# Feed-forward stages whose first chunk multiplies unnormalised x: a two-block transformer kernel

## What is computed

```python
def rmsnorm(x, g):
    x32 = x.astype(jnp.float32)
    y = x32 * lax.rsqrt(jnp.mean(x32 * x32, axis=-1, keepdims=True) + RMS_EPS)
    return y.astype(x.dtype) * g

def modulate(z, g, shift, scale):
    return rmsnorm(z, g) * (1.0 + scale) + shift

def swiglu(h, wi, wo):
    a, u = jnp.split(h @ wi, 2, axis=-1)
    return (jax.nn.silu(a) * u) @ wo

x = x + 0.5 * m[2] * swiglu(modulate(x, norm_g[l, 0], m[0], m[1]), ffn1_wi[l], ffn1_wo[l])
```

## Time and profile before

| what | value |
|---|---|
| median of 3 runs | 3235.24 us (3233.91 to 3236.90) |
| profiled execution | 3234.64 us |
| its span in the trace | 3232.1 us |
| PE busy | 3152.3 us, 98% of the span |
| DVE busy | 1860.3 us, 58% |
| ACT busy | 1026.0 us, 32% |
| share of PE in the chain that ended last | 89% |

### The profile page before, as it was taken

The page is one execution under the profiler, slowest core; times in us unless marked ns, Lnnn a source line. Parts: engine busy times, 40 slices in busy tenths (PEclk is TensorE's granted clock), DMA queues, the critical chain, the costliest instruction groups (busy, mean ns, idle before and its releaser), DMA issues.

```text
span 3232.1 us, 37291 instructions
## 1 busy us (share of the span) xinstructions
PE 3152.3 (98%) x15190; PEld 2528.8 (78%) x15190; DVE 1860.3 (58%) x2673; ACT 1026.0 (32%) x1480; POOL 10.2 (0%) x23
## 2 busy tenths in 40 slices
PE   8999999998899999999999999999999998899998
PEld 7888888776678888788877888788887764578887
DVE  7876555645555554666646554566665655554444
ACT  4212222345442222322234222332224344332222
POOL 0000000000000000000000000000000000000000
PEclk9999999999999999999999999999999999899999
DMA  6433432210034433255522443235551210123331
GB/s 229 140 118 124 149 125 85 66 44 11 1 124 152 154 124 117 85 207 190 197 92 79 169 144 131 79 118 206 190 178 62 76 55 1 56 91 102 97 98 52
DMA packets 101846, 365.03 MB, mean 113 GB/s; under 512 B 11247, under 2 KB 12543, under 8 KB 101421
## 3 DMA queue, kind: packets, MB, share of 16 engines
q1 hardware_dynamic: 100636, 357.94, 32.4%
q0 software_dynamic: 1040, 4.71, 0.4%
HBM read 360.51 MB, written 2.10 MB: 112 GB/s over the span
## 4 chain that ended last, share of the span: by engine, by line
PE 89%; DVE 6%; ACT 3%; issue 1%; DMA 1%; SPq 0%; POOL 0%; DVEq 0%; ACTq 0%; POOLq 0%
PE ps L192 25%; PE ps L194 25%; PE ps L193 25%; PE ps L196 4%; PE ps L197 2%; DVE SQ L610 1%; PE ps L496 1%; DVE HL L599 1%; DVE WL L184 1%; PE ps L2373 1%; ACT WH L179 1%; PE ps L2606 0%; DVE XT L855 0%; DVE RAW L1317 0%; PE ps L2706 0%
## 5 line engine op out<-in xcount | busy, mean ns | idle before, releaser
L192 PE MATMUL ps<-HH,WH 128*128 128x512 f32 x2464 | 973.8, 395 | 4.2 <-ACT S L769 2.2
L194 PE MATMUL ps<-HH,WL 128*128 128x512 f32 x2464 | 960.9, 390 | 0.0
L193 PE MATMUL ps<-HL,WH 128*128 128x512 f32 x2464 | 960.0, 390 | 0.0
L179 ACT ACTIVATE WH<-RAW 128x1024 fp32r<-128x1024 f32 x456 | 459.1, 1047 | 622.4 <-PE ps L194 366.5
L184 DVE TENSOR_TENSOR WL<-RAW,WH 128x1024 fp32r<-128x1024 f32 x456 | 542.9, 1219 | 92.3 <-ACT WH L179 92.1
L192 PEld LDWEIGHTS ps<-HH,WH 128*128 128x128 f32 x2464 | 462.9, 188 | 116.7 <-issue 9.9
L194 PEld LDWEIGHTS ps<-HH,WL 128*128 128x128 f32 x2464 | 462.7, 188 | 98.7
L193 PEld LDWEIGHTS ps<-HL,WH 128*128 128x128 f32 x2464 | 463.1, 188 | 97.1 <-issue 4.6
L855 DVE SCALAR_TENSOR_TENSOR XT<-ps,DER,XT 128x512 f32<-128x512 f32 x512 | 346.4, 682 | 249.0 <-PE ps L194 234.2
L192 PE MATMUL ps<-GH,WH 128*128 128x512 f32 x1056 | 412.5, 391 | 4.8 <-DVE GL L793 4.8
L194 PE MATMUL ps<-GH,WL 128*128 128x512 f32 x1056 | 411.1, 389 | 0.0
(11 more groups left out here) (356 smaller groups left out, 2467.8 us busy)
## 6 DMA issues: line engine op xcount, KB each, us to landing
RAW<-in_w_modt SPq DMA_DIRECT2D x200, 512.0 KB, 5.0
RAW<-in_ffn_wi SPq DMA_DIRECT2D x176, 512.0 KB, 4.8
RAW<-in_ffn_wo SPq DMA_DIRECT2D x88, 512.0 KB, 4.9
RAW<-in_w_gu SPq DMA_DIRECT2D x88, 512.0 KB, 4.3
RAW<-in_w_in SPq DMA_DIRECT2D x44, 512.0 KB, 3.6
RAW<-in_w_down SPq DMA_DIRECT2D x44, 512.0 KB, 4.2
RAW<-in_w_out SPq DMA_DIRECT2D x16, 512.0 KB, 4.4
STG<-in_w_modt SPq DMA_DIRECT2D x10, 512.0 KB, 12.8
```

The lines of the kernel that those rows point to most:

```text
L179: act.e.activation(u.hi, u.ld.view, ACT.Copy).then_inc(u.hi_done.sem, 1)
L192: pe.e.matmul(out, wh, x[0], start=first, stop=False)
L193: pe.e.matmul(out, wh, x[1], start=False, stop=False)
L194: m = pe.e.matmul(out, wl, x[0], start=False, stop=last)
```

## The change

Before feed-forward stages 2, 3, 5 and 8, chunk 0 no longer waits for the norm. It multiplies x * a (a: the norm's weights times 1 + scale) as soon as each block of x is final, and three things are put right afterwards: the per-token factor R = 1/rms is multiplied on behind PSUM, and the shift b enters as b times the weights, one number for each output feature. All other chunks still use the normalised h.

- `AheadSplit(k)` splits x * a into `UH` (ACT, 128x512) and `UL` (DVE, 128x512). It stands one step behind the addition of block k: in the last `Down` group of stage 2, in `OutMM` of mixers 1 and 7, in `PoolAdd` of mixer 4.
- `Sums` with `full` adds all eight squares on DVE; `Factor` sums over partitions with one float32 product of 128x512 behind block 2 of chunk 0 and runs `Newton` on 128x512. `NormSplit` stands behind it and reads R from SBUF.
- `Up` of chunk 0: DVE multiplies both halves by R, ACT applies SiLU with the bias, DVE adds the other bias and multiplies. Chunk 1 takes the two halves in turns as well.
- `BiasDot`, `BiasSum`, `BiasCopy` make the bias numbers a stage ahead: two more weight loads, eight DVE operations on 128x256, two PE products of one column, an ACT copy.
- `OutMM` uses six banks in place of three, the weights of the following stage are split at d = 5 and 6 in place of both at d = 7.
- In the four stages the condition is spread behind chunks 2 and 3, and the dot products are dealt out from chunk 4 on.
- `RstdSum`, `RstdSpread` and the `Busy` products go at these four places.

```diff
+class AheadSplit(Step):
+    def scalar(self, act):
+        P, k = self.P, self.k
+        act.wait_ge(*self.ready)
+        act.wait_ge(*self.gain)
+        act.e.activation(P.UH[:, k, :], P.XT[:, k, 0:T], ACT.Identity, scale=P.mod_a(self.mi, k)).then_inc(self.hi.sem, 1)
+    def vector(self, dve):
+        P, k = self.P, self.k
+        dve.wait_ge(*self.hi)
+        dve.e.scalar_tensor_tensor(P.UL[:, k, :], P.XT[:, k, 0:T], P.mod_a(self.mi, k), P.UH[:, k, :].bitcast(F32),
+                                   ALU.mult, ALU.subtract).then_inc(self.lo.sem, 1)
+class Factor(Step):
+    def sum(self, pe):
+        P = self.P
+        pe.wait_ge(*self.total)
+        pe.wait_ge(*self.bankfree)
+        pe.e.matmul(P.banks[7], P.ONE, P.SA[:, 0:T], start=True, stop=True).then_inc(self.summed.sem, 1)
+class BiasDot(Step):
+        for k in range(8):
+            w, b = self.view[:, :, k * 128:(k + 1) * 128], P.mod_b(self.mi, k)
+            if k == 0:
+                dve.e.tensor_scalar(P.ACC, w, b, None, ALU.mult).then_inc(self.part[k].sem, 1)
+            else:
+                dve.wait_ge(*self.part[k - 1])
+                dve.e.scalar_tensor_tensor(P.ACC, w, b, P.ACC, ALU.mult, ALU.add).then_inc(self.part[k].sem, 1)
...
 (Up.tensor)
+                    if self.factor and k == 2:
+                        self.factor.sum(pe)
...
 (Up.scalar)
+                if q == 0 and self.factor:
+                    act.wait_ge(*self.scaled[q])
+                    act.wait_ge(*self.biased)
+                    act.e.activation(s, s, ACT.Silu, bias=P.BIAS[:, q:q + 1]).then_inc(self.silu[n].sem, 1)
...
 (Up.vector)
+                if self.factor:
+                    d = F.S[:, 1, :] if q else s
+                    dve.wait_ge(*self.done[q, n])
+                    dve.wait_ge(*self.factor.done)
+                    dve.wait_ge(*self.sfree[n])
+                    dve.e.tensor_tensor(d, out, self.factor.R, ALU.mult).then_inc(self.scaled[q].sem, 1)
+                    if q:
+                        dve.wait_ge(*self.silu[n])
+                        dve.wait_ge(*self.scaled[q])
+                        dve.wait_ge(*self.biased)
+                        dve.e.scalar_tensor_tensor(s, d, P.BIAS[:, q:q + 1], s, ALU.add, ALU.mult).then_inc(self.mul[n].sem, 1)
...
 (OutMM)
-        self.b = d % 3
+        self.b = (0, 1, 2, 4, 5, 6, 4, 5)[d]
...
 (ffn)
+            if ahead:
+                self.downfree = NONE
+                F = Ffn(self, ctx, mi, segs, self.norm_tiles(ctx, False))
+                R = self.sb(ctx, self.name("RB"), [128, T], F32)[:, :]
+                units, self.units = self.units, self.split([wi[1], wi[NF + 1]])
+                F.factor = self.add(Factor(self, R))
+                self.add(NormSplit(self, mi, segs, F.h, after, R=R))
+                self.add(Up(F, 0, units))
...
                     for d in range(8):
                         self.add(DownPart(down, d))
+                        if nxt is not None and last and d:
+                            self.add(AheadSplit(self, nxt, d - 1, down.evac[d - 1, 0][0]))
...
 (out_products)
+        for d in range(8):
+            ahead = self.split([w[d + 1]]) if d < 7 else None
+            if d in (5, 6):
+                later += self.split([following[d - 5]])
+            job(d)[1](units)
+            units = ahead
...
+                if d == 1:
+                    bias["lds"] = self.bias_loads(wi)
+                elif d == 2:
+                    bias["dot"] = self.add(BiasDot(self, nxt, bias["lds"]))
...
 (mixer_pool)
-            self.add(Busy(self, 4))
             last = add(3)
+            self.add(SumsEnd(sums))
+            self.add(AheadSplit(self, mi + 1, 7, last.evac))
```

More of the change, by code:

```diff
@@ L408, in late @@
     def late(self, dve, k):
-        if 1 < k < 7:
+        if 1 < k < (9 if self.full else 7):
             P, w, j = self.P, self.w, k - 1
@@ new lines, with __init__, vector @@
+class BiasDot(Step):
+    def __init__(self, P, mi, lds):
+        self.P, self.mi, self.lds = P, mi, lds
+        self.before, self.shift = P.biased, P.modt[mi, 0]
+        self.part = [P.s["bias_dve"].next() for _ in range(8)]
+        self.summed = P.s["bias_mm"].next()
+        for ld in lds:
+            ld.users = [self.part[7]]
+        at = [ld.slot for ld in lds]
+        lo, step = min(at), abs(at[0] - at[1])
+        self.view = P.RAW[:, lo:lo + step + 1:step, :]
+        self.order = [at.index(lo), 1 - at.index(lo)]
+    def vector(self, dve):
+        P = self.P
+        for ld in self.lds:
+            dve.wait_ge(*ld.landed)
+        dve.wait_ge(*self.before)
+        dve.wait_ge(*self.shift)
+        for k in range(8):
[5 more added lines that the diff above has]
+                dve.e.scalar_tensor_tensor(P.ACC, w, b, P.ACC, ALU.mult, ALU.add).then_inc(self.part[k].sem, 1)
@@ new lines, with __init__, tensor, scalar @@
+class BiasSum(Step):
+    def __init__(self, dot, bank=7):
+        self.dot, self.bank = dot, bank
+    def tensor(self, pe):
+        P, dot = self.dot.P, self.dot
+        pe.wait_ge(*dot.part[7])
+        for i, q in enumerate(dot.order):
+            m = pe.e.matmul(P.banks[self.bank][:, 508 + q:509 + q], P.ACC[:, i, :], P.ONE[:, 0:1], start=True, stop=True,
+                            skip_group_check=True)
+        m.then_inc(dot.summed.sem, 1)
+class BiasCopy(Step):
+    def __init__(self, dot, bank=7):
+        self.dot, self.bank = dot, bank
+        dot.P.biased = self.done = dot.P.s["bias_act"].next()
+    def scalar(self, act):
+        P = self.dot.P
+        act.wait_ge(*self.dot.summed)
+        act.e.activation(P.BIAS, P.banks[self.bank][:, 508:510], ACT.Copy).then_inc(self.done.sem, 1)
@@ L3043, in norm_split, with bias_loads, ffn @@
         return h
-    def ffn(self, mi, segs, wi, wo, after, following, blk=None, rows=(), early=()):
+    def bias_loads(self, w):
+        return [self.add(LoadStep(Load(self, src))).ld for src in (w[0], w[NF])]
+    def ffn(self, mi, segs, wi, wo, after, following, blk=None, rows=(), early=(), ahead=False, nxt=None, dot=None):
         with self.scope() as ctx:
@@ L3182, in add @@
             def add(g):
-                return [self.add(PoolAdd(self, mi, means[g], o, bfree, sums)) for o in range(2)][1]
+                for o in range(2):
+                    k = 2 * g + o
+                    adds[k] = self.add(PoolAdd(self, mi, means[g], o, bfree, sums))
+                    if k:
+                        self.add(AheadSplit(self, mi + 1, k - 1, adds[k - 1].evac))
+                return adds[k]
             prod(0)
```

138 lines of the change are left out of this document (107 added, 31 removed).

## The result

| what | before | after |
|---|---|---|
| median, runs of the same chip | 3235.37 us (3233.91 to 3236.90, 4 runs) | 3252.65 us (3250.44 to 3255.11, 4 runs) |
| profiled execution, its span | 3234.64 us, 3232.1 us | 3255.11 us, 3253.3 us |
| PE, DVE, ACT busy | 3152.3, 1860.3, 1026.0 us | 3140.5, 1914.0, 1047.9 us |

The account below looks back on a forecast made before the run. PE, busy 98% of the span, bounds the kernel. Chunk 2 starts +2.3, bias products +1.9, `OutMM` waits +5.1 and clock +11.8 make +21 on 3234.6: 3255.7, with 0.6 for the median 3256 us; range 3232 to 3272.

Parts of the forecast that it names:

- The start of a stage: DVE's chain sets chunk 2's start: gains of 3.1 us in stage 2 and 4.3 us in stage 8.
- the 7.2 us: DVE's list from the end of `NormSplit` to chunk 2's first weight rest: R products, table load, SiLU, product, copy, rest, `Diag`.
- The load of the table: SiLU's table load on ACT stands in the chain to chunk 2's weights: 1.28 us a stage, bound 0.
- The end of stage 2: Last group becomes a loop through ACT and DVE, 2.72 us a step; chunk 2 of stage 3 loses 5.5 us.
- the 4.2: Loss in us in mixer 4 from the same loop: chunk 2 of stage 5 at 1747.2 against 1743.0.
- Bias: Bias products on PE +1.9 us (0.5 a stage); `BiasDot` makes PE wait 2.5 us in each `OutMM`, +5.1.
- The clock: Half clock behind PE's new waits at chunk 2 and in `OutMM`: +11.8 us, bounds 0 and 18.
- Clock holds: Rival: PE's clock doesn't fall behind the new waits; sum +9 us, 3244; chance 0.15.
- DVE isn't late: Rival: ACT's and DVE's steps overlap better, third chunk earlier; +1 us, further branch 3228; chance of faster 0.13.
- the full gain: 36 us at four boundaries less new sums and bias, 3205; needs chunk 2's weights ahead of the norm on DVE.
- No change: Rival: gains of mixers and losses of stages cancel, clock falls twice; +2 to +7 us; chance 0.17.
- much slower: Rival: SiLU's table wait, stage 3 DVE-bound by four dot products, clock falls of 3.3 each; +38 us, 3273; chance 0.1.

Follow-up runs that it names:

- rounding first: Changed kernel with ACT's rounding of block d-1 moved ahead of its square of block d at all places of `AheadSplit`: 3236.51 us, 1.0000 of the kernel before.
- `Diag` later: Changed kernel with the 128x1024 product of `Diag` moved behind chunk 1's own DVE work in stages 2, 3 and 5: 3250.13 us, 1.0044 of the kernel before.
- bias in halves: Changed kernel with `BiasDot`'s eight operations split four and four behind d = 2 and d = 3 in mixers 1 and 7: 3249.01 us, 1.0035 of the kernel before.
- the first filling: Changed kernel with 14, 8, 10, 12 `Busy` ahead of chunk 2 (stages 2, 3, 5, 8) and 8 at `OutMM` d = 4: 3248.37 us, again 3248.98.
- the table early: Changed kernel with a one-column SiLU behind each `Factor`'s root on ACT, so the table loads during Newton's steps: 3243.00 us, 1.0023 of the kernel before.

## Why the prediction was right

Forecast 3256 us, measured 3252.65: within the range, and in the band from 3247 to 3266 that had the largest chance. Each large term was tested by an edit of its own.

**The start of a stage.** The chain on DVE is as laid out, and so are its ends. From the start of stage 2's first products (940.72) chunk 2 starts 27.9 us later, forecast 27.8. In stage 3, on the prediction's zero (1291.4, and 6.24 later in this trace), at 50.6 against 50.7. In stage 5 at 1759.61, and 1747.2 plus the 11.9 us by which stage 3's landmark is later gives 1759.1. Stage 8: 27.1 (2899.60 less 2872.47) against 26.6. Every one is within 0.6 us. The waits themselves were less well placed: 4.8, 2.6, 3.7 and 4.0 against 5.1, 5, 5 and 3.9. In stages 3 and 5 half clock and the sum's product (2.08 us for two instructions at half clock) delay PE within the wait, which the prediction named as a thing that shortens it, and costs nothing. Removing that early stall (rounding first) brought the waits of stages 3 and 5 to 5.09 and 5.07, the forecast's 5. The listed members of the 7.2 us add up to 7.5 and the small waits; 7.2 holds because the second product with R runs beside the table's load, as the trace has it (1340.86 for two, the load at 1341.61).

**The load of the table.** Counted exposed at 1.28 a stage, against a bound of 0: 1.09 to 1.28 by the run that moves it. The load stood behind the wait for DVE at 1341.61 and SiLU follows it by 1.30 us, start to start, without a further drain: the trace of after bears out what the earlier trace rows showed.

**The end of stage 2.** Step 2.73 us (forecast 2.72), bank wait 1.17 (1.8), sum's wait 5.82 (6.2). For stage 5 the prediction expected about 6 us as well, and it is 2.61, because PE arrives there later, behind its waits for `Z` and for a bank. The cause, a loop through ACT by the order of its list, is shown by the run that turns two of ACT's instructions round. In mixer 4 the same loop also makes `Z` late, 3.68 us in place of 1.6, which the prediction didn't list; it is part of the 4.2 that it gave there as a start of chunk 2.

**Bias.** Two waits of 2.61 (2.5), the four instructions of the two products 0.50 us (0.5). No PE wait for any of the added loads stands in the view. Nor did the four dot products a chunk make anything late that the waits show: those for `GL` between 885 and 2600 us are 3.9 us in all, against 3.8 before.

**The clock** is the one term that was mis-sized: 11.8 forecast, about 8 measured (8.0 by windows, 8.2 to 8.9 by filling the waits). Nearly all of that is `OutMM`: 2.5 us each were put there, and it cost 1.6 in mixer 1 and nothing in mixer 7. The four places at chunk 2 cost 6.4 in place of 6.8, but otherwise spread than forecast (3.0, 0, 1.7, 1.7 for 2.2, 1.2, 1.2, 2.2). I had taken a fall for granted at all six; at two of them, in mixer 7 and in stage 3, none came. With 8 in its place the sum is +2.3 + 1.9 + 5.1 + 8 = 17.3, which is the difference measured; that it fits to the tenth is chance, since the interval is nearly 6 us to either side. It is also chance that the two profiled executions differ by 21.2 us, the forecast's own +21: 3.0 of it lie in parts that weren't changed.

**PE's busy time** fell by 12 us and not by 30. The forecast left out that a product at half clock lasts longer and counts as busy, here behind the sums and the waits, and that the new sums (2.08 us in stage 3) and bias products come on top. By lines, the old sums, the spreading and `Busy` take 34.6 us less than before. The new sums add 5.7 and the bias products some 2, and half clock lengthens other products by some 12: 8 behind the waits and, by the windows, 4.5 behind the sums of stages 3 and 5. That gives a fall of about 15, an estimate; nothing in the time's sum rested on it.

**The rivals.** "Clock holds" gave 3244, and that is the time of the kernel whose waits are filled (3244.5): right on price, but not what happens by itself. "DVE isn't late" falls by the waits. Its further branch, that the order of steps excludes the full gain and that this would be 3205, came out at 3206.4 when the order was changed, with the weights behind the norm and not ahead of it as the prediction asked. "No change" (+2 to +7 us) and "much slower" (+38) both lie outside the interval measured, +12 to +23.

**What stays open.** How far the clock falls in the mixers varies from one run of the same kernel to the next, and what sets it wasn't tried. Nine runs of the changed kernel lie between 3250.4 and 3257.1. In the twelve profiled executions of the changed kernel and its edits, PE comes to its last wait for `PT` in mixer 1 at 883.9 to 889.4 us (886.0 before), though nothing ahead of it differs between them. So a difference of 3 to 5 us between two medians, as with `Diag` later, bias in halves and the first filling, shows an edit's effect only together with its waits. The surplus of the table early over its waits (about 5 us), and 3 us of that of rounding first, are not shown to be the edits' own. The 1.4 and 1.6 us that the changed kernel lost in unchanged parts are taken for such scatter.

## What to carry to other kernels

When a change takes work off the engine that bounds and gives it to another, lay out that other engine's whole list between two needs of the bounding engine, table loads and rounding loops with it, and ask of each next operand: what stands ahead of it that doesn't have to? Here the same operations (but for four SiLU of one column) in the order of the change cost 0.54%, and reordered (next weights first, table loaded while idle, the loop's rounding ahead of its square, a long run of small operations cut in two) they gained 0.98%. Judge such an edit by where the next operand's first product starts, counted from a fixed place: the wait ahead of it also changes with when PE arrives. A short wait of a fully loaded PE costs its length and, often but not each time, 1.6 to 3.0 us of half clock behind it: sum both, and expect the second to scatter.

## What the runs showed of the chip

- A `Busy` of one 128x256 float32 product is two instructions and takes 0.44 us (28 in 6.20 us at clock 1.00); I had reckoned 0.25, and so filled 4.8 us of waiting with 6.2 us of work.
- A fall of the clock behind a wait is not certain: behind 2.61 us in `OutMM` of mixer 1 it came in the changed kernel and not in `Diag` later with the same wait, nor behind the 2.61 us at 2850.12 in mixer 7. Behind 2.48 us in stage 3 it came in `Diag` later, and not behind 2.59 in the changed kernel. Where it came in the changed kernel it cost 1.6 to 3.0 us.
- A change of ACT's table cost its load of 1.28 us and nothing more: SiLU starts 1.30 us behind the load's start at 1341.61. Whether that is on PE's path is a matter of where the load stands: moving it off shortened four waits by 1.09 to 1.28 us.
- Half clock while PE has to wait anyway costs nothing: in stage 3 PE ran at half clock from the sum at 1324.05 on (the first 4 us below), and chunk 2 still started when DVE's chain let it, 50.6 us behind the zero where 50.7 was forecast.

```profile
1324.00:1328.00 4.00, 3.95 (x7) 2.50 (x8) 3.97 (x5) 1.80 (x3) 0.00 (x0) 0.50 0.29 68
```
